# The head of a diffusion layer: x is loaded between the first and the second modulation block, turned before scale and shift are known, and modulated in place

## The reference

```
s_lat, s_ctx = silu(c), silu(c_ctx)                     # two vectors of 1024
mod_lat = split(s_lat @ ada_w + ada_b, 6)               # ada_w is 1024 x 6144
mod_ctx = split(s_ctx @ ada_w[:, :2048] + ada_b[:2048], 2)
h_lat = rms_norm(x,   g0) * (1 + mod_lat[1]) + mod_lat[0]
h_ctx = rms_norm(ctx, g0) * (1 + mod_ctx[1]) + mod_ctx[0]
proj  = h @ w_in                                        # 1024 x (3072 + 1024 + 32)
```

## Time and profile before

| | us |
|---|---|
| median of 3 runs | 1482.08 (1481.82 to 1483.15) |
| the profiled execution, its own time | 1480.8 |
| its span in the profile | 1479.0 |
| PE busy | 1302.7 (88%) |
| DVE busy | 762.0 (52%) |
| ACT busy | 479.0 (32%) |
| share of PE in the chain that ended last | 59% |
| mean granted TensorE clock | 0.948 of full |

### The profile page before, as it was taken

One profiled execution on the slowest core, in us unless ns is written; L12 is line 12 of the kernel. 1 busy time (PEld: TensorE's weight loads), 2 busy tenths in 40 slices (PEclk: granted clock), 3 DMA queues, 4 the chain that ended last, 5 costly groups with the idle time before them and its releaser, 6 DMA issues.

```text
span 1479.0 us, 13899 instructions
## 1 busy us (share of the span) xinstructions
PE 1302.7 (88%) x5053; PEld 757.3 (51%) x5053; DVE 762.0 (52%) x1079; ACT 479.0 (32%) x1115; POOL 232.4 (16%) x207
## 2 busy tenths in 40 slices
PE   6898998989999999889999969997079999999971
PEld 1444454445545555589989834454034444444430
DVE  1238888978893667577777745563900011001041
ACT  1723542561311222556667623343011110110140
POOL 0001320221000000155554300000010110110121
PEclk9899999999999999999999989998579999999985
DMA  8511544425315110256665654433659999999876
GB/s 305 173 29 50 172 150 143 130 79 180 101 42 157 29 29 20 57 164 172 188 190 188 198 204 154 152 140 109 256 173 356 325 337 341 332 329 337 295 223 147
DMA packets 175274, 264.63 MB, mean 179 GB/s; under 512 B 49069, under 2 KB 91814, under 8 KB 175206
## 3 DMA queue, kind: packets, MB, share of 16 engines
q1 hardware_dynamic: 151286, 204.32, 41.6%
q0 software_dynamic: 14416, 52.96, 12.1%
q10 hardware_dynamic: 9504, 6.45, 1.4%
HBM read 214.47 MB, written 49.22 MB: 178 GB/s over the span
## 4 chain that ended last, share of the span: by engine, by line
PE 59%; DMA 13%; ACT 10%; DVE 10%; issue 4%; SPq 1%; POOL 1%; POOLq 0%; DVEq 0%; ACTq 0%
PE ps L1737 26%; PE ps L1062 12%; PE ps L1081 6%; DMA arena<-g_dram 5%; DMA y_dram<-arena 3%; DMA arena<-zt_dram 2%; PE ps L1026 2%; ACT arena L512 2%; PE ps L1634 2%; PE ps L375 2%; ACT arena L521 1%; PE ps L1688 1%; DVE arena L2046 1%; PE ps L1658 1%; DVE arena L568 1%
## 5 line engine op out<-in xcount | busy, mean ns | idle before, releaser
L1737 PE MATMUL ps<-arena 128*128 128x512 f32 (+1 forms) x1120 | 444.7, 553 | 0.0
L1737 PEld LDWEIGHTS ps<-arena 128*128 128x128 f32 x1120 | 211.9, 192 | 208.5 <-issue 203.3
L1062 PE MATMUL ps<-arena 128*128 128x512 f32 x512 | 228.0, 599 | 1.4 <-ACT arena L1178 1.4
L2046 DVE SCALAR_TENSOR_TENSOR arena<-arena,taps 128x1024 f32<-128x1024 f32 x160 | 213.5, 1334 | 5.7
L1062 PEld LDWEIGHTS ps<-arena 128*128 128x128 f32 x512 | 97.2, 193 | 117.3 <-issue 115.3
L375 PE MATMUL ps<-arena 128*128 128x128 f32 x1080 | 133.7, 279 | 19.1 <-DVE arena L592 15.8
L375 PEld LDWEIGHTS ps<-arena 128*128 128x128 f32 x1080 | 128.9, 193 | 25.6 <-DVE arena L592 19.1
L1341 DVE TENSOR_TENSOR arena<-arena,ps 128x512 f32<-128x512 f32 x16 | 11.0, 687 | 213.4 <-PE ps L1062 213.4
L1026 PE MATMUL ps<-arena 128*128 128x512 f32 x256 | 116.3, 610 | 4.6 <-ACT arena L1127 4.6
L1081 PE MATMUL ps<-arena 128*128 128x512 f32 x256 | 115.6, 606 | 4.9 <-DVE arena L1351 4.9
L1026 PEld LDWEIGHTS ps<-arena 128*128 128x128 f32 x256 | 48.7, 195 | 62.7 <-issue 56.2
(11 more groups left out here) (287 smaller groups left out, 1621.5 us busy)
## 6 DMA issues: line engine op xcount, KB each, us to landing
arena<-exp_w_gate SPq DMA_DIRECT2D x16, 2048.0 KB, 11.3
arena<-exp_w_up SPq DMA_DIRECT2D x16, 2048.0 KB, 8.9
arena<-exp_w_down SPq DMA_DIRECT2D x16, 2048.0 KB, 11.1
arena<-ada_w POOLq DMA_DIRECT2D x16, 1024.0 KB, 6.6
arena<-w_in SPq DMA_DIRECT2D x28, 512.0 KB, 4.0
arena<-ada_w SPq DMA_DIRECT2D x4, 2048.0 KB, 10.6
arena<-x SPq DMA_DIRECT2D x16, 512.0 KB, 8.9
arena<-g_dram SPq DMA_DIRECT2D x16, 512.0 KB, 4.6
```

The lines of the kernel that those rows point to most:

```text
L1062: last = mm(ps[gu_bank[s] + j][:], xsT[s][:, k, :], ew[s][j][:, k, :], start=(k == 0), stop=(k == KD - 1))
L1737: last = mm(ps[3 * (m % 2) + gi][:, 0:w], wring[(m + 1) % NW][:, k, :], hT[:, k, o:o + w], start=(k == 0), stop=(k == KD - 1))
L2046: ins = v.scalar_tensor_tensor(accg, cin_l[ci % 2][:, j // 3:j // 3 + GR, j % 3:j % 3 + GW], tp[:, j:j + 1], accg, ALU.mult, ALU.add)
```

## The change

It touches the head only. `N_VROWS` is 7, the number of small loads that fill `vrows`. In the diff, longer runs of removed lines are cut to their first line; they stand in the listing above.

- **Loads.** SP issues ada_w's first block ahead of everything, then the five short rows, then x and ctx, then the other three blocks. The seven loads of `vrows` move to ACT's queue, ahead of silu; ACT's loads of taps and router weights move behind its ten squares.
- **Modulation on PE** (`ada(b)`). The operands change places: 128 x 128 of ada_w are the stationary operand and the two columns of silu_c the moving one. For each block 4 column groups x 8 matmuls = 32 matmuls (64 records), 128 in all in place of 32. The result is in columns at once. The row buffer, its four copies on DVE and the 16 turnings go.
- **Order on PE.** `ada(0)`, `x_turned(0)`, `x_turned(1)`, `ada(1)`, `x_turned(2)`, `ada(2)`, `ada(3)`, then the gates. Five banks (`XB = (4, 5, 6, 7, 0)`) hold the turned steps.
- **x.** DVE scales the tiles as their roots come. It also copies the 8 turned steps of the first group out of PSUM; ACT copies those of the other two.
- **Scale and shift** are applied in place on `hT`, by rows of 128 channels over all tokens (1024 latent and 256 context columns apart): the even k on DVE, the odd ones on ACT, the first four k after the third block, the others after the fourth.
- **Gates on PE.** The loop over k is outside, that over the three parts inside, and each k waits for its row only.

```diff
--- before.py
+++ after.py
@@ -133,7 +133,7 @@
         CIN0 = at[0]
         cin_l = [take(GP).rearrange("p (r c) -> p r c", c=GW + 2) for _ in range(2)]
         cin_c = [take(TC + 2) for _ in range(2)]
-        mrow = arena[0:2, at[0]:at[0] + 2 * D]
+        squares = arena[:, at[0]:at[0] + D]
         cacc = [take(TA) for _ in range(2)]
         ctmp = take(TA)
         STG0 = at[0]
...
@@ -1464,19 +1467,19 @@
         @block.sync
         def _(sp_):
-            for dst, src in small:
...
+            def ada_load(b):
                 sp_.dma_start(aring[b % 3], ada_k[:, :, b * 512:(b + 1) * 512])\
                     .then_inc(sem(f"ada_in{b % 3}"), 16)
+            ada_load(0)
+            for dst, src in small[N_VROWS:]:
+                sp_.dma_start(dst, src).then_inc(sem("small_in"), 16)
             for t in range(NT):
                 src = x_t[t] if t < NL else ctx_t[t - NL]
                 sp_.dma_start(xall[:, t, :], src).then_inc(sem(f"tile_in{t // 2}"), 16)
+            for b in range(1, NAB):
+                if b >= 3:
+                    sp_.wait_ge(sem("ada_used"), b - 2)
+                ada_load(b)
             sp_.dma_start(wring[0][:, :, 0:NGATE], w_k[:, :, OFF_GATE:OFF_GATE + NGATE]).then_inc(sem("w_in0"), 16)
             def batch_loads():
@@ -1625,36 +1628,47 @@
             nc.tensor.matmul(ps[1][:, 0:56], ones[0:1, :], srow[0:1, :], start=True, stop=True)\
                 .then_inc(sem("vT"), 1)
-            pe.wait_ge(sem("silu_c"), 2)
-            for b in range(NAB):
+            pe.wait_ge(sem("head_a"), 2)
+            def ada(b):
                 pe.wait_ge(sem(f"ada_in{b % 3}"), 16 * (b // 3 + 1))
-                if b >= 2:
-                    pe.wait_ge(sem("vcols"), 2 + b - 1)
-                for k in range(KD):
-                    last = nc.tensor.matmul(ps[2 + b % 2][0:2, :], silu_c[:, k, :], aring[b % 3][:, k, :],
-                                            start=(k == 0), stop=(k == KD - 1))
+                for j in range(4 * b, 4 * b + 4):
+                    for k in range(KD):
+                        last = mm(ps[1 if b == NAB - 1 else 2][:, 2 * j:2 * j + 2], aring[b % 3][:, k, (j % 4) * P:(j % 4 + 1) * P],
+                                  silu_c[:, k, :], start=(k == 0), stop=(k == KD - 1))
                 last.then_inc(sem("ada_used"), 1)
-            pe.wait_ge(sem("vcols"), 2 + NAB)
...
+            def x_turned(g):
+                t0, nt = XG[g]
                 pe.wait_ge(sem("xn"), t0 + nt)
                 for k in range(KD):
-                    if n >= 4:
-                        pe.wait_ge(sem("hT"), n - 3)
+                    n = g * KD + k
+                    if len(XB) <= n < len(XB) + KD:
+                        pe.wait_ge(sem("head_v"), n - len(XB) + 1)
+                    elif n >= len(XB) + KD:
+                        pe.wait_ge(sem("head_a"), 2 + n - len(XB) - KD + 1)
                     for i in range(nt):
-                        last = nc.tensor.transpose(ps[4 + n % 4][:, i * P:(i + 1) * P],
-                                                   xall[:, t0 + i, k * P:(k + 1) * P], ident[:])
+                        last = tr(ps[XB[n % len(XB)]][:, i * P:(i + 1) * P], xall[:, t0 + i, k * P:(k + 1) * P], ident[:])
                     last.then_inc(sem("vT"), 1)
-                    n += 1
-            pe.wait_ge(sem("hT"), n)
+            ada(0)
+            x_turned(0)
+            x_turned(1)
+            ada(1)
+            x_turned(2)
+            ada(2)
+            ada(3)
             pe.wait_ge(sem("w_in0"), 16)
-            for gi, (o, w) in enumerate(parts_of(0)):
-                for k in range(KD):
+            for k in range(KD):
+                if k % 2 == 0:
+                    pe.wait_ge(sem("head_v"), KD + k // 2 + 1)
+                else:
+                    pe.wait_ge(sem("head_a"), 2 + 2 * KD + k // 2 + 1)
+                for gi, (o, w) in enumerate(parts_of(0)):
                     last = nc.tensor.matmul(ps[3 + gi][0:NGATE, 0:w], wring[0][:, k, 0:NGATE], hT[:, k, o:o + w],
                                             start=(k == 0), stop=(k == KD - 1))
             last.then_inc(sem("w_used"), 1)
@@ -1764,30 +1778,34 @@
         @block.scalar
         def _(act):
             a = nc.scalar.activation
-            act.dma_start(taps[:], taps_k).then_inc(sem("taps_in"), 16)
-            act.dma_start(rw[:], rw_k).then_inc(sem("taps_in"), 16)
+            for dst, src in small[:N_VROWS]:
+                act.dma_start(dst, src).then_inc(sem("small_in"), 16)
             act.wait_ge(sem("vcols"), 2)
             for j, v0 in enumerate((V_C, V_CC)):
-                nc.scalar.activation(silu_c[:, :, j], vcols[:, v0:v0 + KD], ACT.Silu).then_inc(sem("silu_c"), 1)
+                nc.scalar.activation(silu_c[:, :, j], vcols[:, v0:v0 + KD], ACT.Silu).then_inc(sem("head_a"), 1)
             for t in range(NT):
                 act.wait_ge(sem(f"tile_in{t // 2}"), 32)
-                nc.scalar.activation(hflat[:, t * D:(t + 1) * D], xall[:, t, :], ACT.Square,
+                nc.scalar.activation(squares, xall[:, t, :], ACT.Square,
                                      accum_out=ssq[:, t:t + 1]).then_inc(sem("rms"), 1)
                 act.wait_ge(sem("rms"), 2 * t + 1)
                 nc.scalar.activation(rstd[:, t:t + 1], ssq[:, t:t + 1], ACT.Sqrt, scale=1.0 / D, bias=eps1[:])\
                     .then_inc(sem("rms"), 1)
-            act.wait_ge(sem("vcols"), 2 + NAB + 1)
-            n = 0
-            for t0, nt in XG:
-                j = 0 if t0 < NL else 1
+            act.dma_start(taps[:], taps_k).then_inc(sem("taps_in"), 16)
+            act.dma_start(rw[:], rw_k).then_inc(sem("taps_in"), 16)
+            for g, (t0, nt) in list(enumerate(XG))[1:]:
                 for k in range(KD):
-                    act.wait_ge(sem("vT"), 3 + n + 1)
-                    nc.scalar.activation(hT[:, k, t0 * P:(t0 + nt) * P], ps[4 + n % 4][:, 0:nt * P], ACT.Identity,
-                                         bias=mods[:, k, j:j + 1], scale=gain1[:, k, j:j + 1])\
-                        .then_inc(sem("hT"), 1)
-                    n += 1
+                    n = g * KD + k
+                    act.wait_ge(sem("vT"), 2 + n + 1)
+                    a(hT[:, k, t0 * P:(t0 + nt) * P], ps[XB[n % len(XB)]][:, 0:nt * P], ACT.Copy).then_inc(sem("head_a"), 1)
+            act.wait_ge(sem("head_v"), KD)
+            act.wait_ge(sem("head_a"), 2 + 2 * KD)
+            for k in range(1, KD, 2):
+                act.wait_ge(sem("vcols"), 3 + k // 4)
+                for j, part in ((0, slice(0, T)), (1, slice(T, TA))):
+                    last = a(hT[:, k, part], hT[:, k, part], ACT.Identity, bias=mods[:, k, j:j + 1], scale=gain1[:, k, j:j + 1])
+                last.then_inc(sem("head_a"), 1)
             act.wait_ge(sem("w_used"), 1)
             for gi, (o, w) in enumerate(parts_of(0)):
                 last = nc.scalar.activation(ctmp[0:NGATE, o:o + w], ps[3 + gi][0:NGATE, 0:w], ACT.Copy)
@@ -1946,23 +1964,43 @@
             dve.wait_ge(sem("vT"), 2)
             v.tensor_copy(vcols[:], ps[0][:, 0:NV]).then_inc(sem("vcols"), 1)
             v.tensor_copy(sbc[:], ps[1][:, 0:56]).then_inc(sem("vcols"), 1)
-            for b in range(NAB):
...
+            def normed(t):
                 dve.wait_ge(sem("rms"), 2 * t + 2)
                 link(v.reciprocal(rstd[:, t:t + 1], rstd[:, t:t + 1]))
                 v.tensor_scalar(xall[:, t, :], xall[:, t, :], rstd[:, t:t + 1], None, ALU.mult)\
                     .then_inc(sem("xn"), 1)
-            dve.wait_ge(sem("vT"), 3 + KD * len(XG) + 1)
+            for t in range(4):
+                normed(t)
+            for k in range(KD):
+                if k % 2 == 0:
+                    normed(4 + k // 2)
+                dve.wait_ge(sem("vT"), 2 + k + 1)
+                v.tensor_copy(hT[:, k, 0:4 * P], ps[XB[k % len(XB)]][:, 0:4 * P]).then_inc(sem("head_v"), 1)
+            for t in range(8, NT):
+                normed(t)
+            dve.wait_ge(sem("vcols"), 2)
+            for b, j0, j1, bank in ((NAB - 1, 0, 12, ps[2]), (NAB, 12, 16, ps[1])):
+                dve.wait_ge(sem("ada_used"), b)
+                n, k0, k1 = j1 - j0, (0 if j0 == 0 else 4), j1 - KD
+                link(v.tensor_tensor(mods[:, j0:j1, :], bank[:, 2 * j0:2 * j1].rearrange("p (j w) -> p j w", w=2),
+                                     vcols[:, V_AB + j0:V_AB + j1].unsqueeze(2).to_broadcast([P, n, 2]), ALU.add))
+                v.scalar_tensor_tensor(gain1[:, k0:k1], mods[:, KD + k0:KD + k1, :], 1.0,
+                                       vcols[:, V_NG + k0:V_NG + k1].unsqueeze(2).to_broadcast([P, k1 - k0, 2]),
+                                       ALU.add, ALU.mult).then_inc(sem("vcols"), 1)
+                dve.wait_ge(sem("vcols"), 3 + k0 // 4)
+                if k0 == 0:
+                    dve.wait_ge(sem("head_v"), KD)
+                    dve.wait_ge(sem("head_a"), 2 + 2 * KD)
```

(21 more changed lines are left out.)

## The result

| | before | after |
|---|---|---|
| median | 1481.82 us (1478.55 to 1483.15, 5 runs) | 1496.40 us (1491.31 to 1500.02, 5 runs) |
| profiled span | 1479.0 us | 1498.3 us |
| PE starts the gates at | 66.45 us | 79.53 us |
| mean granted clock of that run | 0.948 | 0.934 |

The ratio is 1.010, with a 95% interval from 1.008 to 1.012: slower by 14.6 us of the medians, where 13.6 were forecast. The profiled execution is the slowest of the five after the change, 3.6 us above their median.

The account below looks back on a forecast made before the run. The serial head was taken as the bound, PE running without a pause behind it: gates from 66.45 to 79.3 us (+12.85), plus 0.8 for slower gates, +13.6 on 1482.1 gives 1495.7 us; range 1476 to 1502, likeliest case 1489 to 1502.

Parts of the forecast that it names:

- `ada(0)` starts: PE's start on the first modulation block, after small loads landing at 9.0 and silu: at 10.9 us, bounds 9.5 to 12.5.
- `ada(0)`: First modulation block on PE: 64 records at the half clock, 13.6 us, ending at 24.5.
- `x_turned(0)` and the wait for tile 7: PE transposes x's first group, then waits for DVE to scale tile 7: from 24.5 to 32.3 us.
- `x_turned(1)`: PE transposes x's second group, paced by ACT's copies at 0.67 us a step: 5.4 us, ending at 37.7.
- `ada(1)`: Second modulation block: full clock for the first 2.8 us, then half, 10.8 us in all; bounds 6.8 and 13.6.
- `ada(2)`, `ada(3)`: Last two modulation blocks on PE, both at the half clock, their loads hidden: 27.2 us together, ending at 79.3.
- gates longer by: The gates' 48 records start at the half clock and may keep it longer: +0.8 us, bounds 0 and +1.7.
- The clock: In the head, modulation matmuls moving two columns neither raise nor hold PE's clock; bounds 6.8 and 13.6 us a block.
- Hidden steps: Last scale and shift rows, ready 3.2 us after the last block, and ada_w's late part: both covered, cost nothing.
- A: Rival: thin modulation matmuls count like any and the clock is full; gates 9.95 us earlier, 1470.9 us; chance 0.10.
- B: Rival: the clock stays where it is under the modulation blocks, up or down; 1476.0 us; chance 0.09.
- C: Rival: weight loads do not slow with the clock, so each modulation block takes 6.8 us; 1472.9 us; chance 0.02.

Follow-up runs that it names:

- Experiment 1: The changed kernel with each modulation matmul moving 128 columns (silu_c's two repeated) in place of 2: 1476.87 us, 0.9973 of the kernel before.
- Experiment 4: The kernel before with only the modulation's operands exchanged (128 matmuls of 128 x 128 by 2 columns), old order and loads: 1503.06 us, ratio 1.0152.
- experiment 2: The changed kernel with ACT's loads of taps and router weights issued behind its copies of x's turned steps: 1494.74 us, 1.0087 of the kernel before.
- experiment 6: The changed kernel with the late loads of taps and router weights and 16 moving columns in place of 2: 1487.4 us, one execution.
- 7: The changed kernel with the late loads of taps and router weights and 32 moving columns in place of 2: 1498.7 us, one execution.
- experiment 3: The changed kernel with both 128 moving columns and the late loads of taps and router weights: 1472.70 us, 0.9954 of the kernel before.

## Why the prediction was right, step by step

| step | forecast | measured |
|---|---|---|
| `ada(0)` starts | 10.9 | 11.7 |
| `ada(0)` | 13.6 | 13.7 |
| `x_turned(0)` and the wait for tile 7 | 7.8 | 7.7 |
| `x_turned(1)` | 5.4 | 4.6 |
| `ada(1)` | 10.8 | 11.3 |
| `x_turned(2)` | 3.6 | 3.5 |
| `ada(2)`, `ada(3)` | 27.2 | 27.1 |
| gates start | 79.3 | 79.5 |
| gates longer by | 0.8 | 1.0 |
| first projection tile | not priced | +1.7 |

- **The clock.** That the thin stream neither raises nor holds the clock was read from two contrasts in the earlier trace rows. Experiment 1 shows it as the cause: same loads, same instructions, more moved columns, 13 us less in the last two blocks. Experiment 4 shows it without the new order.
- **How long the full clock outlasts x's turning** in `ada(1)` was a guess: 2.8 us, borrowed from an idle stretch. It came to some 2.3 us here, and to some 3.3, 5.0 and 4.5 in experiments 2, 6 and 7. That `ada(1)` is only 0.5 off is in part luck.
- **The start** was 0.8 late: the small loads landed by 9.73, not 9.0. The last was ssm_norm_g, one of the seven on ACT's queue, which the sum had put beside the block at no cost.
- **`x_turned(1)`** was the step with a mechanism missed, and with a term too large. The router weights' issue took 1.91 us in the earlier trace rows, on idle queues; behind ada_w's blocks it took 8.56 and held ACT until 35.4, which cost 0.9 us here (experiment 2). Against that, ACT's plain copies took 0.50 us a step and not 0.67, and without the wait the group took 3.7 us, not 5.4. The two errors have opposite signs, and what is left of them, -0.8, makes up for the start's +0.8: luck. Experiments 1 and 3 give the wait's price under the wide stream: 4.6 us.
- **The first projection tile** was not priced. Behind the same pause of 1.4 us between gates and projection it ran at the full clock in nine of the thirteen profiles (17.4 us) and lost 1.7 us in four: the changed kernel, 128 columns with late loads, 32 and 64 columns. It doesn't follow the clock at which the gates began: that was the half one before and after, the full one in experiment 3 (19.08 us) and in experiment 1 (17.38). Its cause is open. With all of it the forecast of the time, 0.7 us off in medians of which one spreads over 8.7, is closer than its terms were.
- **Hidden steps** stayed hidden: DVE's and ACT's last rows were done by 83.4, 4 us into the gates. The late part of ada_w did no harm: the one load of it that stands in the chain, at 224.76, takes 6.06 us, and 6.60 in the kernel before.
- **The rivals.** A needs that thin matmuls count like any: refuted by 1. B, that the level stays as it is: refuted for 2, 16 and 32 columns, and right for 64. C, that weight loads don't slow down: refuted; 64 records took 13.7 us. The figure of the Trainium skill ("TensorE: Matmul & The Clock Gate", "LDWEIGHTS (loading the stationary operand)"), 128 columns over 1.2, fits the full clock's 0.107 us a record and not the half clock's 0.214. Part 4 of the same page of the Trainium skill, by which transposes do not bring the full clock, disagrees with experiment 6, where it rose from 0.50 to 1.00 over those of `x_turned(2)`.

## What to carry to other kernels

Making the big matrix the stationary operand to multiply it by a few columns costs the same on paper, but here it ran at half the clock: look for a stretch in which PE is fully busy at 0.50, and either keep the wide operand moving or repeat the thin one, which cost nothing here at 128 columns. Judge an order of work apart from the form of the work in it: here the order gained 4 us, 9 with the late loads, and the form lost 22. A load that is issued behind big ones can hold its engine, not only its queue: the router weights' 64 KB held ACT for 8.56 us behind ada_w's blocks, and 1.77 us when issued 24 us later.

## What the runs showed of the hardware

- Keeping and raising the clock were two things here: in the one profile with 64 moving columns the full level stayed over 23 us (37.4 to 60.5, with 16 transposes between), and the first block ran its 13.9 us at the half pace; in both profiles with 128 the pace rose within the first block (9.5 and 9.9 us in place of 13.9).
- The recorded clock says 1.00 until its first change. In experiment 4 it says 1.00 from 15 to 69 us while the records keep the half pace, 0.214 us. Early in an execution the distance between starts is the better witness.
- The widened products cost nothing: at the half pace 64 records took 13.7 us with 2 moving columns and 13.9 with 64; at the full clock they took 7.1 with 64 and 7.1 to 7.2 with 128.
- Open: what happens between 32 and 64 columns, when `x_turned(2)` raises the clock and when not, when the clock falls behind the gates, and why the stretch between the scan and the output projection differs by up to 5.7 us between profiles of the same code there. None of these was tried.
